# The scan of a gated linear attention: one visit for the sums of squares, and two levels moved beside two others

## The reference

```
qh = silu(split(q));  fgate = lb + (1 - lb) * sigmoid(split(f_pre))
o  = hgrn2_chunk_scan(qh, 1 - fgate, split(i), log(fgate))
     # S_t = diag(f_t) S_{t-1} + k_t v_t^T,  o_t = S_t^T q_t, per head (8 heads of 128)
o  = rms_norm(o, norm_g) * silu(split(g))    # mean of squares over a head's 128 columns
```

## Time and profile before

| what | value |
|---|---|
| median of 3 runs (lowest, highest) | 906.63 us (906.29, 906.78) |
| profiled execution | 907.01 us |
| its span, first to last instruction | 905.2 us |
| PE busy | 892.1 us, 99% of the span |
| DVE, ACT, POOL busy | 678.3, 469.4, 202.1 us |
| chain that ended last, PE's share | 95% |
| mean granted TensorE clock | 0.999 |

### The profile page before, as it was taken

How to read it: one execution, slowest core, us unless ns; L and a number is a source line. 1 busy time by engine, 2 the same in 40 slices (tenths; PEclk the granted TensorE clock), 3 DMA queues, 4 the chain that set the end, 5 groups by cost and what they waited for, 6 DMA issues and landing times.

```text
span 905.2 us, 16787 instructions
## 1 busy us (share of the span) xinstructions
PE 892.1 (99%) x6759; PEld 790.7 (87%) x6759; DVE 678.3 (75%) x1286; ACT 469.4 (52%) x942; POOL 202.1 (22%) x111
## 2 busy tenths in 40 slices
PE   8999999999999999999999999999999999999997
PEld 7879999889999888888888899887888888888886
DVE  7745987587556888776676778858888888788885
ACT  7444337575354674444435657776554445543443
POOL 4123421631222110653214522220100211210100
PEclk9999999999999999999999999999999999999999
DMA  8356352154334646555554364215355555465441
GB/s 327 118 185 228 138 185 94 47 210 140 112 122 140 234 165 233 208 174 221 186 191 181 140 223 174 93 62 209 117 200 196 186 183 203 172 230 189 164 162 47
DMA packets 23182, 153.67 MB, mean 170 GB/s; under 512 B 2865, under 2 KB 3249, under 8 KB 5569
## 3 DMA queue, kind: packets, MB, share of 16 engines
q1 hardware_dynamic: 22384, 150.43, 46.4%
q0 software_dynamic: 576, 2.10, 0.7%
q10 hardware_dynamic: 144, 0.07, 0.0%
HBM read 151.28 MB, written 1.05 MB: 168 GB/s over the span
## 4 chain that ended last, share of the span: by engine, by line
PE 95%; DVE 3%; ACT 1%; DMA 1%; issue 0%; SPq 0%; DVEq 0%
PE pb L531 93%; PE pb L534 2%; DMA sm<-in_sm 1%; DVE X L546 0%; DVE FA L540 0%; ACT FA L537 0%; DVE wl L540 0%; DVE st L543 0%; ACT R L537 0%; DVE FA L549 0%; DVE R L546 0%; SPq L570 0%; DVE wh L555 0%; ACT wh L537 0%; DVE FA L543 0%
## 5 line engine op out<-in xcount | busy, mean ns | idle before, releaser
L531 PE MATMUL pb<-R,wh 128*128 128x256 f32 (+2 forms) x2224 | 545.7, 325 | 1.8 <-ACT R L537 1.1
L531 PE MATMUL pb<-R,wl 128*128 128x256 f32 (+1 forms) x1512 | 420.3, 281 | 0.0
L531 PEld LDWEIGHTS pb<-R,wh 128*128 128x128 f32 x2224 | 369.5, 189 | 41.6 <-issue 1.4
L540 DVE TENSOR_TENSOR wl<-raw,wh 128x1024 fp32r<-128x1024 f32 (+1 forms) x207 | 273.5, 1345 | 78.8 <-ACT wh L537 77.2
L540 POOL TENSOR_TENSOR wl<-raw,wh 128x1024 fp32r<-128x1024 f32 (+1 forms) x71 | 173.0, 2440 | 594.3 <-ACT wh L537 445.9
L531 PEld LDWEIGHTS pb<-R,wl 128*128 128x128 f32 x1512 | 283.6, 188 | 1.7
L537 ACT ACTIVATE wh<-raw 128x1024 fp32r<-128x1024 f32 (+1 forms) x223 | 226.0, 1044 | 54.9 <-PE pb L531 39.9
L531 PE MATMUL pb<-wh,R 128*128 128x512 f32 (+1 forms) x704 | 227.0, 389 | 0.1
L531 PEld LDWEIGHTS pb<-wh,R 128*128 128x128 f32 x704 | 131.7, 188 | 31.1 <-issue 1.7
L537 ACT ACTIVATE FA<-pb 128x256 f32<-128x256 f32 (+7 forms) x240 | 93.8, 414 | 114.7 <-PE pb L531 103.6
L531 PE MATMUL pb<-wl,R 128*128 128x512 f32 (+1 forms) x352 | 135.5, 385 | 0.0
(11 more groups left out here) (131 smaller groups left out, 464.1 us busy)
## 6 DMA issues: line engine op xcount, KB each, us to landing
raw<-in_w SPq DMA_DIRECT2D x137, 1024.0 KB, 4.8
X<-in_x SPq DMA_DIRECT2D x2, 512.0 KB, 4.2
raw<-in_w SPq DMA_DIRECT2D x2, 512.0 KB, 7.1
post<-in_ffn_post SPq DMA_DIRECT2D x2, 512.0 KB, 4.1
post<-in_w POOLq DMA_DIRECT2D x2, 512.0 KB, 4.0
FA<-in_w POOLq DMA_DIRECT2D x2, 512.0 KB, 7.3
out<-X SPq DMA_DIRECT2D x4, 256.0 KB, 2.0
cst<-in_cst SPq DMA_DIRECT2D x1, 821.5 KB, 12.6
```

What stands on the lines that cost most here:

```text
L531: return self.real.matmul(*a, **k) if self.real else self
L540: return self.real.tensor_tensor(*a, **k) if self.real else self
```

## The change

It has two parts. The four `ssq` steps become one, behind the last read, with eight matmuls: heads 0 to 3 on the four column pieces, then heads 4 to 7 on the same ones. To keep all squares until then, they go to `SQ`, 2048 columns that lie over all of `Tt` and the first 16 columns of the bounds; their activation now waits for the last decays in place of the former sum. And in the string of the scan, level (1, 0) comes directly behind level (0, 1) instead of ahead of tile hg 3, and level (1, 1) directly behind level (0, 2) instead of behind tile hg 7.

```diff
-    segs.append(("scan", p.take(), [metas, scan(0), scan(1), *lats, read(0) + read(1)]))
+    segs.append(("scan", p.take(), [metas, scan(0), scan(1), *lats, [("read", g, i) for g in range(2) for i in range(2)] + [("ssq",)]]))
...
-    "scan": "..abc.aabc..bb.c..ab.bc...a.b.b..cc...bcb.c..a..cc...bc.b.ca.bbcd.c..cbcbad.bd.c.e.b.ecf.eff.ff."
-            "ff.f",
+    "scan": "..abc.aabc..bb...abc.bc...a.bc.b..c...bcb.c..a..cc...bc.b.ca.bbcd.c..cbcbad.bd.c.e.b.ecf.ef.f.f.f",
...
+        SQ = fa(o - 2032, 2048)
...
                 elif kind == "ssq":
-                    g, i = a
-                    b = bank("ssq", (3,)) if (g, i) == (0, 0) else banks.of("ssq")
-                    e.wait_ge(*act.at(("read", g, i)))
-                    for j in range(2):
-                        h = 4 * g + 2 * i + j
+                    b = bank("ssq", (3,))
+                    for h in range(8):
+                        g, p0 = h // 4, 32 * (h % 4)
 
                         es = cst[:, CO["esel"][0] + 1 - g:CO["esel"][0] + 33 - g]
-                        m = e.matmul(b[32 * (h % 4):32 * (h % 4) + 32, 0:256], es, Tt[1][:, 512 * g + 256 * j:512 * g + 256 * j + 256],
-                                     start=g == 0, stop=g == 1)
-                    m.then_inc(*pe.up(step))
+                        e.wait_ge(*act.at(("read", g, h // 2 % 2)))
+                        m = e.matmul(b[p0:p0 + 32, 0:256], es, SQ[:, 256 * h:256 * h + 256], start=g == 0, stop=g == 1)
+                    m.then_inc(*pe.up("ssq"))
...
                 elif kind == "read":
                     g, i = a
                     e.wait_ge(*pe.at(step))
+                    h0 = 4 * g + 2 * i
+                    e.wait_ge(*dve.at(("decay", 0, 6)))
+                    e.wait_ge(*dve.at(("decay", 1, 6)))
                     e.wait_ge(*dve.at(("state", g)))
-                    e.wait_ge(*pe.at(("ssq", g, 0)) if i else pe.at(step))
-                    e.activation(Tt[1][:, 512 * g:512 * g + 512], banks.of(step)[:, :], ACT.Square).then_inc(*act.up(step))
+                    e.activation(SQ[:, 256 * h0:256 * h0 + 512], banks.of(step)[:, :], ACT.Square).then_inc(*act.up(step))
```

More of the change, by code:

```diff
@@ L273, in scan @@
         return s
-    def read(g):
-        return [x for b in range(2) for x in (("read", g, b), ("ssq", g, b))]
     metas = [("meta", j) for j in range(4)] + [("meta_turn", g) for g in range(2)] + [("meta_state", g) for g in range(2)]
     lats = [[("lat", w, i) for i in range(3)] for w in ("ck", "cq")]
-    segs.append(("scan", p.take(), [metas, scan(0), scan(1), *lats, read(0) + read(1)]))
+    segs.append(("scan", p.take(), [metas, scan(0), scan(1), *lats, [("read", g, i) for g in range(2) for i in range(2)] + [("ssq",)]]))
     for n in range(8):
@@ L1810, in vector @@
                         if name == "qpe":
-                            e.wait_ge(*pe.at(("ssq", 1, 1)))
+                            e.wait_ge(*pe.at("ssq"))
                         e.wait_ge(*pe.at(use))
```

## The result

The changed kernel takes 908.83 us (median; the kernel before takes 906.70 on the same chips). The ratio is 1.0021, with a 95% interval of 1.0014 to 1.0028: about 2.1 us slower. The forecast was 906.8, with a range up to 907.6, so the time lies outside it, on the slow side. The profiled execution took 909.32 us around a span of 907.5, against 907.01 around 905.2 before: 2.3 us more span.

What follows compares the result with a forecast made beforehand. TensorE, busy 89.20 of 89.20 us between 88 and 177.2 us, was taken as the bound. -1.81 (sums) - 0.62 (merges) + 2.58 (wait) = +0.15 on 906.63 gave 906.8 us, range 904.2 to 907.6.

Steps and rivals of the forecast that it cites:

- Part 1's size: Sums of squares, four TensorE visits into one: three visits saved, -2.25, the fourth longer, +0.44; together -1.81 us.
- the other reading: Visit of the sums: a matmul's second pass holds back its neighbour's first; eight matmuls need nine rounds, term -0.71.
- The merges: Levels (1, 0) and (1, 1) beside (0, 1) and (0, 2): each saves 0.31 us of piece-mode entry and exit, both 0.62.
- The wait: TensorE at level (1, 2) waits for decay (1, 1), whose last instruction is caught behind GpSimd: +2.58 us.
- the second residue: GpSimd's residue after tile ckv 0, forecast to ask at 118.84 instead of 119.46 and to run 119.35 to 121.6.
- the third instruction: VectorE's last instruction of decay (1, 1), 256 elements, forecast to take 2.6 instead of 0.41, ending at 121.9.
- Rival B: At decay (1, 1) the third instruction gets in ahead of GpSimd; TensorE waits 0.35 to 0.4; 904.6 us; chance 0.20.
- the two rows that the prediction gave for it: GpSimd asking during a VectorE instruction: at 699.41 the next VectorE instruction took 2.89, not 0.68; at 94.58 GpSimd took 3.16, not 2.40.
- The price of the wait: After level (1, 2) all engines shift with TensorE, which has no wait of its own up to 177.2; price +2.58 us.
- "No new wait" behind part 1: At the sums: the last squares end at 175.86, 0.7 before the last visit, so the moved sums wait for nothing new.
- Forecast A: At decay (1, 1) the third instruction is caught behind GpSimd; 906.8 us, own range 906.4 to 907.3; chance 0.66.

Runs made afterwards that it cites:

- the repaired kernels: Changed kernel with GpSimd's residue after tile ckv 0 made by VectorE (905.31 us; banks as before 904.44), or waiting for decay (1, 1), banks as before (904.55).

## Why the prediction was wrong, step by step

**Part 1's size: right.** Forecast -1.81. The visit of the sums takes 1.00 to the next gemm matmul (forecast 0.99), and in the changed kernel TensorE's shift falls by 1.8 there; with the banks as before the kernel is 1.88 ahead at 316 us. The two passes of neighbouring pieces run side by side, as the earlier trace rows had it: 16 records in 1.00. By the other reading, nine rounds, the visit would have lasted 2.1. (The -0.71 given for that reading counts nine rounds against two; by the same reading the present visit of two matmuls has three, and the term would have been -0.93. Nothing else hangs on it.)

**The merges: right.** Forecast 0.31 each, 0.62 together. At the visit before the wait TensorE stands at 118.92 instead of 119.43, 0.59 ahead with the 0.08 at the head. Level (1, 0) alone is worth 0.26 in the distance.

**The wait: right in place, cause and size.** Forecast: the second residue asks at 118.84, the third instruction at 119.25, ends at 121.9, and TensorE waits to 121.95. Measured: 118.94, 119.34, 121.90 and 121.96. Rival B, the third instruction ahead of GpSimd, had 0.20 and is what the repaired kernels do. The rule of the Trainium skill named there ("SBUF — State Buffer", section "Who interferes with whom"), that the one issued first holds the other off for the whole instruction, agrees: 2.56 for the third instruction when GpSimd is 0.4 ahead, 0.41 when GpSimd is behind. Of the two rows that the prediction gave for it, is a cast with one SBUF input, of which that rule as quoted says nothing; the instruction with two inputs, for which it was needed, is shown here.

**The price of the wait: wrong, and this is the first step that failed.** The prediction said of the time after the wait that "all engines wait for TensorE again and shift with it", so that a wait of 2.58 costs 2.58. It took every matmul behind the wait at the duration that the trace of before shows, from an execution in which TensorE never stood still in the scan. What stood in its place: behind 2.3 us of idle time TensorE's granted clock was 0.50 for 3.4 us, which cost another 1.5; with TensorE kept busy in the same wait the clock stayed and the distance fell by 1.32. The Trainium skill ("TensorE: Matmul & The Clock Gate", section "HAM oscillation — how this bites in real kernels") has the mechanism, for waits on transfers that are longer than this one: they send TensorE back to its lower clock, and the work behind them starts slow. The trace agrees in the fall to 0.50. It differs in that a wait of 2.31 was enough, and in that the work behind it started at full clock and became slow 1.6 us later; and behind the wait of 2.30 with level (1, 1) merged the clock stayed at 1.00. The measurement decides.

**"No new wait" behind part 1: wrong, the second step that failed.** That sentence followed only the squares, from ScalarE to the last sum. It did not follow what the moved step takes, bank 3, and who gets the banks after it. The queue of TensorE showed kn 7 in another bank than before; what it cost, 0.55, was to be had from the trace of before: its last evacuation of kn runs 183.45 to 183.85, half a microsecond behind the 183.35 at which `kv_group` starts.

**The sum.** Forecast -1.81 - 0.62 + 2.58 = +0.15. Measured for the same three together about +0.1 (1.89 - 1.8), and with the two missing terms, 1.5 and 0.55, +2.1. Forecast A had the right wait for the right reason and still missed the time. Had both terms been there, the forecast would have been 906.63 + 2.2 = 908.8.

**A better version.** Three kernels beat both: the levels as in the change with the second residue behind decay (1, 1) or on VectorE, or only level (1, 0) merged, each with the banks of kn kept. They take 904.4 to 904.7, ratios 0.9976 to 0.9978, 2.0 to 2.3 us below the kernel before, and can't be told apart. The simplest of them is the last, which moves no engine's work. Part 1 with the banks kept and no merge at all, 904.84, is simpler still, and by the medians not told apart from the last either.

## What to carry to other kernels

Price a wait of TensorE by its length and by what the clock does behind it: a wait of 2.3 us cost between 2.3 and 4.9 us in the profiled executions here, wait and slow stretch together (4.9 is 2.3 and the 2.6 that +2.72 leaves beside +1.89 and -1.8). When a step moves, follow everything that it takes (the bank that a least-recently-used rule gives it, and the holders behind it) as well as what it reads and writes. And where VectorE and GpSimd both read two SBUF operands, the order of their requests is part of the schedule: one semaphore wait that put GpSimd behind VectorE took the changed kernel, banks as before, from 908.48 to 904.55.

## What was not expected of the hardware

- TensorE's clock at an idle time of 2.3 us: four profiled executions with the same wait (2.30 or 2.31) and no other work in it showed four things. The granted clock was 0.50 for 3.4 us, from 1.6 us behind the end of the wait; for 3.4 us, from 0.3 behind it; for 6.8 us, from half a microsecond ahead of its end; and it did not fall at all. The length of the wait alone does not tell which; what decides is not settled here.
- In the slow stretch a matmul of 272 columns took 0.227 us between starts, against 0.126 at full clock: a little less than double.
- A GpSimd residue that was asked for while a VectorE instruction ran took 2.93 and 2.68 instead of 2.39; the VectorE instruction of 512 columns caught behind it took 2.90, the one of 256 columns 2.56, instead of 0.68 and 0.41. In both cases what it took was the rest of GpSimd's instruction and 0.3 to 0.55 more.
